# Query norms applied inside the exponential, and attention software-pipelined one block behind three pairs of score banks

## The reference, cut to what matters

```python
def qkv_heads(x, g_norm, p):
    qkv = rms_norm(x, g_norm) @ p['w_qkv']
    q, k, v = jnp.split(qkv, [N_HEADS * HEAD_DIM, (N_HEADS + N_KV) * HEAD_DIM], axis=-1)
    q = rms_norm(q.reshape(bsz, t, N_KV, GQ, HEAD_DIM), p['q_norm'])
    k = rms_norm(k.reshape(bsz, t, N_KV, HEAD_DIM), p['k_norm'])
...
def sink_softmax(s, valid, sink):
    m = jnp.maximum(jnp.max(s, axis=-1, keepdims=True), sink)
    e = jnp.exp(s - m)
    return e / (jnp.sum(e, axis=-1, keepdims=True) + jnp.exp(sink - m))
...
    s = jnp.einsum('bnqkgd,bnskd->bnkgqs', qc, kb) * SCALE     # 64-frame chunk sees itself and the one before
    pr = sink_softmax(s, valid, sink)
    o = jnp.einsum('bnkgqs,bnskd->bnqkgd', pr, vb)
    y = x + o @ p['w_out']
```

## Time and profile before

| what | value |
|---|---|
| median of 3 runs | 1814.18 us (1810.55 to 1814.22) |
| the profiled execution's own time | 1818.81 us |
| its span | 1817.1 us, mean granted TensorE clock 0.933 |
| PE busy | 1654.3 us (91%) |
| DVE, ACT, POOL busy | 727.7, 295.9, 599.8 us |
| chain that ended last | PE 83%, DVE 8%, POOL 3% |

### The profile page before, as it was taken

The page is one execution under the profiler, slowest core; times in us unless marked ns, Lnnn a source line. Parts: engine busy times, 40 slices in busy tenths (PEclk is TensorE's granted clock), DMA queues, the critical chain, the costliest instruction groups (busy, mean ns, idle before and its releaser), DMA issues.

```text
span 1817.1 us, 33445 instructions
## 1 busy us (share of the span) xinstructions
PE 1654.3 (91%) x14584; PEld 1578.1 (87%) x14584; DVE 727.7 (40%) x1256; ACT 295.9 (16%) x483; POOL 599.8 (33%) x356
## 2 busy tenths in 40 slices
PE   6997875887887999999999999976899999999999
PEld 6996764776776999999999999954799999999999
DVE  6645676666664542200222112867243310022100
ACT  3001222221222221100111001133121200012000
POOL 2433234243202333334333343222033433334332
PEclk9997776889997999999999999976699999999999
DMA  7540001000003344444444444430044444444442
GB/s 291 169 162 14 8 16 24 2 15 15 2 15 124 116 142 159 149 152 138 141 160 149 152 139 139 139 116 1 8 156 139 138 139 155 152 156 138 146 161 98
DMA packets 41609, 201.58 MB, mean 111 GB/s; under 512 B 13888, under 2 KB 15040, under 8 KB 19008
## 3 DMA queue, kind: packets, MB, share of 16 engines
q1 hardware_dynamic: 19232, 96.89, 15.4%
q0 software_dynamic: 12528, 91.23, 15.0%
q10 hardware_dynamic: 9744, 11.88, 2.2%
HBM read 192.82 MB, written 6.37 MB: 110 GB/s over the span
## 4 chain that ended last, share of the span: by engine, by line
PE 83%; DVE 8%; POOL 3%; issue 2%; ACT 2%; DMA 1%; ACTq 1%; SPq 0%; DVEq 0%; POOLq 0%
PE PS L587 20%; PE PS L588 20%; PE PS L589 20%; PE PS L562 3%; PE PS L564 3%; PE PS L563 3%; PE PS L680 2%; PE PS L650 2%; PE PS L841 1%; PE PS L620 1%; PE PS L664 1%; PE PS L855 1%; PE PS L859 1%; POOL EE L518 1%; PE PS L611 1%
## 5 line engine op out<-in xcount | busy, mean ns | idle before, releaser
L412 POOL TENSOR_TENSOR WL<-WR,WH 128x2048 fp32r<-128x2048 f32 x87 | 405.7, 4663 | 459.0 <-DMA WH<-in_w 449.5
L587 PE MATMUL PS<-HH,WH 128*128 128x320 f32 x1344 | 416.8, 310 | 3.7 <-POOL WL L412 2.0
L589 PE MATMUL PS<-HH,WL 128*128 128x320 f32 x1344 | 415.9, 309 | 0.0
L587 PE MATMUL PS<-XH,WH 128*128 128x320 f32 x1120 | 347.2, 310 | 0.4
L589 PE MATMUL PS<-XH,WL 128*128 128x320 f32 x1120 | 346.1, 309 | 0.0
L588 PE MATMUL PS<-XL,WH 128*128 128x320 f32 x1120 | 346.1, 309 | 0.0
L588 PE MATMUL PS<-HL,WH 128*128 128x320 f32 x896 | 276.9, 309 | 0.0
L587 PEld LDWEIGHTS PS<-HH,WH 128*128 128x128 f32 x1344 | 252.9, 188 | 5.6 <-issue 3.2
L589 PEld LDWEIGHTS PS<-HH,WL 128*128 128x128 f32 x1344 | 253.0, 188 | 0.0
L587 PEld LDWEIGHTS PS<-XH,WH 128*128 128x128 f32 x1120 | 210.3, 188 | 1.4 <-issue 1.1
L588 PEld LDWEIGHTS PS<-XL,WH 128*128 128x128 f32 x1120 | 210.3, 188 | 0.3
(11 more groups left out here) (389 smaller groups left out, 2295.9 us busy)
## 6 DMA issues: line engine op xcount, KB each, us to landing
WH<-in_w POOLq DMA_DIRECT2D x87, 1024.0 KB, 5.2
WR<-in_w SPq DMA_DIRECT2D x87, 1024.0 KB, 4.9
X<-in_xT SPq DMA_DIRECT2D x8, 320.0 KB, 11.0
out<-X ACTq DMA_DIRECT2D x8, 320.0 KB, 5.0
UR<-UF ACTq DMA_DIRECT2D x16, 80.0 KB, 4.2
UF<-UR SPq DMA_DIRECT2D x64, 20.0 KB, 1.8
WR<-in_wglu SPq DMA_DIRECT2D x1, 1024.0 KB, 4.9
S<-in_s ACTq DMA_DIRECT2D x4, 256.0 KB, 2.6
```

Of the source, the lines that this page charges most:

```text
L412: nc.gpsimd.tensor_tensor(WL[:, r], WR[:, r], WH[:, r].bitcast(F32), ALU.subtract).then_inc(w_split, 2)
L587: mm(out, wh[:, k, wc], xh[:, k, cols], start=(k == 0), stop=False)
L589: last = mm(out, wl[:, k, wc], xh[:, k, cols], start=False, stop=(k == kt - 1))
```

## The change

- The query norm is no longer multiplied into the queries. Their weight goes into the copy of the keys (`KD`), and one over their root into the `scale` operand of the exponential, with a table `RQ` of 20 columns for each of four pairs of query tiles. All query sums take the narrow form (`query_sums`), beside the projection, the last pair after it. For the samples the scale is spread by `query_back` and multiplied in `sample_queries`.
- The value tiles move ahead of the queries in the projection, and their transposes into slot 2 and behind it (`value_rows`).
- `exps` reads the scores from PSUM: four activations of 128 columns, each with a scale and a bias that are columns in SBUF and a sum output (`accum_out`), in place of one of 512. DVE no longer writes the shifted scores, nor reduces the sums. The multiplication by the reciprocal goes from POOL to DVE.
- Scores rotate over three pairs of banks (4/5, 0/1, 2/3); transposes have bank 6 alone and outputs bank 7 alone. PE's turn becomes values of block i-3, transposes of block i-2, scores of block i. The sample blocks stand between prompt blocks 13, 14 and 15.
- `X` is written to DRAM and read back after the attention; `PT`, `VW` and `VS` lie in its room.
- POOL copies the new sample keys, and then loads and splits the weight slot 52, which before it did ahead of the attention.

```diff
-QKV_TILES = [8, 9, 0, 1, 2, 3, 4, 5, 10, 11, 6, 7]
+QKV_TILES = [8, 9, 10, 11, 0, 1, 2, 3, 4, 5, 6, 7]
+ATT_ORDER = list(range(14)) + [16, 14, 17, 15]
...
@@ GpSimd
-            for r in range(AO % 2 + 2):
-                split(r % 2, AO // 2 + r // 2, True)
-            for u in range(UNITS):
-                pool.wait_ge(sm_inv, u + 1)
-                gt(e, e, SM[:, u % 2, 5, 0:ng].unsqueeze(2).broadcast_to((P, ng, kk)), M).then_inc(sm_p, 1)
+            split(0, AO // 2, True)
+            split(1, AO // 2, True)
+            new_keys()
+            split(0, AO // 2 + 1, True)
...
@@ TensorE
+            def query_sums(p):
+                pe.wait_ge(qk_sq, 2 * p + 4)
                 for m in range(2):
                     for t in range(5):
                         at = 10 * m + 2 * t
+                        last = mm(PS[:, 2, at:at + 2], SC[:, m, t * P:(t + 1) * P], BD[:, 0:P:64], start=True, stop=True)
+            def attend(i):
+                if i >= 3:
+                    values(i - 3)
+                if i >= 2:
+                    transposes(i - 2)
+                scores(i)
+            def qkv_attention():
+                slot_as_ready("qkv", XH, XL, KT, xn_wait(3), range(KT), 2)
+                slot("qkv", 1, 1, XH, XL, KT, between=key_sums)
+                slot("qkv", 2, 2, XH, XL, KT, between=lambda n: value_rows(0, NCH if n == 1 else 0))
+                value_rows(NCH, NCH + NB)
+                for i in range(3, N_QKV):
+                    slot("qkv", i, i, XH, XL, KT, between=lambda n: query_gap(i - 3, n))
+                query_sums(3)
+                attend(0)
+                attend(1)
+                query_back()
+                for i in range(2, UNITS):
+                    attend(i)
...
@@ ScalarE
+            def exps(i):
+                act.wait_ge(sm_sub, i + 1)
+                if u < 16:
+                    fn(sm[3][:, 0:4], sm[2][:, 0:4], ACT.Exp)
+                    for g in range(4):
+                        c = 10 * (g % 2) + 2 * (u % 4) + g // 2
+                        last = fn(ee(i)[:, g * P:(g + 1) * P], PS[:, b0 + g // 2, (g % 2) * P:(g % 2 + 1) * P], ACT.Exp,
+                                  bias=sm[1][:, g:g + 1], scale=RQ[:, u // 4, c:c + 1], accum_out=sm[4][:, g:g + 1])
+                    last.then_inc(sm_exp, 1)
...
+                act.wait_ge(unit_done, end_unit("qkv"))
                 act.dma_start(KS[:, :, :, 0:CH], ckT).then_inc(cache_in, 16)
-                act.dma_start(VS[0:CH, :, :], cv).then_inc(cache_in, 16)
+                for k in range(UNITS):
+                    if k >= 3:
+                        out_high(k - 3)
+                    if k >= 2:
+                        transposed(k - 2)
+                    exps(k)
...
+                for k in range(KT):
+                    act.dma_start(X[:, k], XD[:, k]).then_inc(x_in[k], 16)
...
@@ VectorE, less_max and over_sum
                 o(v.tensor_reduce(sm[0], ps, AX.X, ALU.max))
-                o(tt(sm[1], sm[0], sink, ALU.max))
-                tt(sm[2], sink, sm[1], S_)
-                tt(e, ps, sm[1].unsqueeze(3).broadcast_to(shape), S_).then_inc(sm_sub, 1)
+                if u < 16:
+                    o(tt(sm[0], sm[0], RQ[:, u // 4].rearrange("p (a t h) -> p t h a", a=2, h=2)[:, u % 4], M))
+                o(stt(sm[1], sm[0], -1.0, sink, M, ALU.min))
+                if u < 16:
+                    tt(sm[2], sm[1], sink, S_).then_inc(sm_sub, 1)
...
-                o(v.tensor_reduce(sm[4], e, AX.X, A))
                 o(tt(sm[4], sm[4], sm[3], A))
-                v.reciprocal(sm[5], sm[4]).then_inc(sm_inv, 1)
+                o(v.reciprocal(sm[5], sm[4]))
+                tt(e, e, sm[5].unsqueeze(3).broadcast_to(shape), M).then_inc(sm_p, 1)
```

More of the change, by code:

```diff
@@ L589, in slot @@
                             last = mm(out, wl[:, k, wc], xh[:, k, cols], start=False, stop=(k == kt - 1))
-                    last.then_inc(unit_done, 1)
+                        if between:
+                            if h == 1:
+                                last.then_inc(unit_done, 1)
+                            between(2 * j + h)
+                    if not between:
+                        last.then_inc(unit_done, 1)
             def stage(name, xh, xl, kt, wait=None, order=None, L=None):
@@ new lines, in out_high, with qkv_attention @@
+            def out_high(i):
+                act.wait_ge(pv_done, i + 1)
+                ps, dst = o_tiles(i, XHB)
+                fn(dst, ps, ACT.Copy).then_inc(o_hi, 1)
+            def qkv_attention():
+                square(0)
+                square(1)
+                act.wait_ge(x_spilled, 16 * KT)
+                act.wait_ge(xn_lo, 4 * KT)
+                act.dma_start(VS[0:CH, :, :], cv).then_inc(cache_in, 16)
+                key_root(0)
+                key_root(1)
+                value_rows(0, NCH)
+                square(2)
+                value_rows(NCH, NCH + NB)
+                square(3)
+                act.wait_ge(qk_ready, 2)
@@ L1512, in out_high @@
-            def out_high(u):
-                act.wait_ge(pv_done, u + 1)
-                ps, dst = o_tiles(u, XHB)
-                fn(dst, ps, ACT.Copy).then_inc(o_hi, 1)
-            def attention():
-                for i in range(UNITS + 2):
-                    if i < UNITS:
-                        exps(i)
-                    if i >= 2:
-                        out_high(i - 2)
-                    if 0 <= i - 1 < UNITS:
-                        transposed(i - 1)
+                for p in range(3):
+                    query_root(p)
+                    square(4 + 2 * p)
+                    square(5 + 2 * p)
@@ new lines, in out_low, with qkv_attention @@
+            def out_low(i):
+                dve.wait_ge(o_hi, i + 1)
+                ps, dst = o_tiles(i, XLB)
+                _, hi = o_tiles(i, XHB)
+                tt(dst, ps, hi.bitcast(F32), S_).then_inc(o_lo, 1)
+            def qkv_attention():
+                dve.wait_ge(unit_done, unit0("qkv"))
+                v.memset(VP[:, :, 0:CH], 0.0).then_inc(v_pad, 1)
+                qkv_evac(0)
+                qkv_evac(1)
+                qkv_evac(2)
+                key_norm(0)
+                qkv_evac(3)
+                key_norm(1)
+                dup_keys()
+                qkv_evac(4)
+                qkv_evac(5)
+                for p in range(3):
+                    query_inv(p)
+                    qkv_evac(6 + 2 * p)
+                    qkv_evac(7 + 2 * p)
+                query_inv(3)
+                less_max(0)
+                less_max(1)
+                over_sum(0)
+                sample_queries()
+                for k in range(2, UNITS):
+                    if k >= 3:
+                        out_low(k - 3)
+                    less_max(k)
+                    over_sum(k - 1)
+                over_sum(17)
+                out_low(15)
+                out_low(16)
+                out_low(17)
```

380 lines of the change are left out of this document (181 added, 199 removed).

## The result

The changed kernel takes 1823.7 us (median of 5 timed runs, 1822.01 to 1828.35) against 1814.18 for the kernel before. The ratio is 1.0062, 95% interval [1.0043, 1.008]: slower, by 8 to 15 us. Forecast was 1816, no measurable difference. The changed kernel is slower in both.

What follows compares the result with a forecast made beforehand. TensorE alone bounds the projection; in the attention no engine is full and a loop of waits sets the turn. Projection end 1195.2 + attention 100.6 + block 3.7 = 1299.5 against 1297.4, +2: forecast 1816 us, range 1804 to 1825.

Steps and rivals of the forecast that it cites:

- Projection, +5: Projection, TensorE full: wide head sums out -6.45, narrow sums in +7.2, value transposes in +4.3; together +5.0 us.
- Head, -13: From T, the last projection matmul, to the first block's weights: 10.1 us against 23.1 before.
- One turn, 4.69 or 4.34: One attention turn: 4.69 us at TensorE's lower clock, 4.34 at the higher, about 4.6 mixed, against 4.02 before.
- loop A: Turn's loop through maximum, sum, transposes and scores: 4.69 us at the lower clock, 3.75 at the higher.
- loop B: Turn's loop through maximum, exponentials, ACT's high half and DVE's low half: 4.34 us, the longer loop at the higher clock.
- The sum of the attention, 100.6: Preparation and attention: 104.4 us at the lower clock, 100.6 with a quarter of the time higher, against 107.2 before.
- clock higher: Rival, attention: more turns at the higher clock and POOL's split out of the way, -7 us, 1807; chance 0.17.
- The one-time block, +3.7: First attention turns: POOL's split of slot 52 holds a DVE instruction with SBUF operands; +3.7 us, bounds 0 to 5.
- At nothing: Spill and return of `X`, stores of keys and values, `new_keys` on POOL: no cost; a late return at most 5 us.
- the exponentials are no bound: Rival, attention turns: costlier sum outputs make the exponentials the bound, deciding from 2.45 us; 1823; chance 0.20.
- `KS` does not hold ACT: Rival, head: the load of `KS` by itself holds ACT's queue for 8.02 us; +6 us, 1822; chance 0.11.
- The turn did not stay at 4.02: Rival, attention: loops overlap better than drawn and the turn stays at 4.02 us; 9 us come back, 1807; chance 0.12.

Runs made afterwards that it cites:

- e5_halves: Changed kernel with each twenty query head-sum matmuls cut into two halves of ten, an output tile apart: 1818.35 us, ratio 1.0014 to the kernel before.
- e4_one_sum: Changed kernel with one 20-column matmul standing for each twenty head sums of the three query tiles inside the projection: 1815.71 us, ratio 0.9993 to the kernel before.
- e8_order_late: Changed kernel with TensorE's and DVE's turns reordered and POOL's split of slot 52 held until the last values, head sums whole: 1789.99 us, ratio 0.9854.
- e1_split_late: Changed kernel with POOL's load and split of slot 52 held until the values of the 17th block are done: 1815.95 us, ratio 0.9998.
- e2_scores_ahead: Changed kernel with TensorE taking values, scores, transposes, so scores stand ahead of transposes, plus one wait: 1811.48 us, ratio 0.997 to the kernel before.
- a2_again: The changed kernel timed once more, unaltered, beside the kernel before: 1820.99 us, ratio 1.003.
- e3_turn_order: Changed kernel with TensorE taking scores, values, transposes, and DVE taking maximum, sum, low half: 1792.43 us, ratio 0.9862 to the kernel before.
- b1_swap: The kernel before, with the load of `VS` issued ahead of that of `KS`, nothing of the change in it: 1815.53 us, ratio 0.9986.

## Why the prediction was wrong

The mechanisms were mostly right, and the sum came out short because two terms stood on a clock that I had set too high.

- *Projection, +5: the step that failed first.* "TensorE is full here, so its work is added up" counts instructions and assumes that each runs at full speed. The counted part was, if anything, too high: three sums out (-6.45), three in (19 matmuls in 2.12 on the chain, 2.13 for twenty, +6.4), value rows 1.96 + 1.86 = 3.8 for the 4.3 that I took. That is +3.8, and `e5_halves`, with the same matmuls and no fall of the clock, measured +4.0. Put at nothing were one or two falls of the clock at 1.5 us: +5.3 to +6.8 in all, measured 5.6 and 7.1. `e4_one_sum` and `e5_halves` show it. No row of before could show it: the only narrow sums there, line 1073 in the earlier trace rows, stand behind the projection, with no full stretch after them. My upper bound of +7 nearly covered the size, but for another reason, late evacuations, that no trace shows.
- *Head, -13:* held. T + 10.1 was forecast for the first block's weights without the block, and `e8_order_late` has 9.9 with the sums at 2.41. Where the sums ran partly at the lower clock, it was 11.3 (`e1_split_late`), which the forecast did not have. The kernel after, with block and slow sums, has 14.5.
- *One turn, 4.69 or 4.34:* loop A held, loop B was too high. 4.62 at the lower clock with exactly the chain of loop A; 3.92 and not 4.34 at the higher one; and `e2_scores_ahead` laid loop B bare at 3.91. The average of 4.60 that came out as forecast has luck in it: fewer turns at the higher clock than assumed, shorter ones there, and the memsets that I had counted apart. The exponentials took 1.97 for the 2.1 forecast, and the low bound of 0.72 was far off. The Trainium skill's 93 ns for each column operand (ScalarE: Activation LUTs, What ACT_TABLE_LOAD costs) had given 0.17 more; the trace is nearer to the row's figure: 0.44 for an activation of 128 columns with two column operands.
- *The sum of the attention, 100.6: the second term that failed.* It took the clock share of before over. Measured were 0.55 in the turns and 0.50 in the tail, where rows 1 had 0.63 and 0.58. From the first weights on my terms give 104.4 - 10.1 = 94.3 us at the lower clock and 90.5 with a quarter of the time high; measured were 91.7, nearly all low. By the same slope the lost share is worth some 2.6 us and the low-clock terms were some 1.4 too high (both estimates), so one error hid half of the other. This miss is also of the size of the spread between executions: with the same turns `a2_again`, `e4_one_sum` and `e5_halves` measured 91.0, 89.2 and 91.2. The rival "clock higher" had used the same lever in the wrong direction. Its condition, 0.70, was met only by the kernels with the order of `e3_turn_order`.
- *The one-time block, +3.7:* held. One small DVE instruction took 4.3 us too long (4.49 less 0.17), of which 3.2 to 4.3 reached the first weights, inside the bound of 5. Five of the seven DVE instructions of a turn have two operands in SBUF, as the prediction counts, and not four as the section on the change has it. The rule of the Trainium skill (SBUF — State Buffer, Who interferes with whom) fits again: an instruction of 4 columns was held until POOL's was done.
- *At nothing:* the return of `X` and the stages behind cost nothing, 519.7 in both.
- *The rivals:* the exponentials are no bound (1.97, it wanted 2.45). `KS` does not hold ACT: its issue took 0.62 in the kernel after, with the table load right behind. The turn did not stay at 4.02.

Added up for the first pair of traces: +2.1 in the projection and +1.9 in preparation and attention beyond the forecast (block 0.6, clock share and the rest of the turns 1.2), and +3.4 ahead of the projection, within the spread. Behind the projection's start the traces have +3.5 and +6.1 where +2 was forecast: the verdict hung on 1.5 to 4 us, nearly all of it the clock. With the falls gone from the projection (`e5_halves`) the ratio is 1.0014 [0.9999, 1.003], which is no measurable difference, as forecast.

## What to carry to other kernels

Where an in-order queue holds work for several blocks, draw the loop through each queue at once. Here only the places of `scores` and `out_low` cost 33 us of a stretch of 106, together with the clock that came with them, far more than any of the parts that the change moved. Work that is added to a full TensorE is not priced by its durations alone: look for what it does to the granted clock behind it, and try a run of very narrow matmuls in parts, as `e5_halves` does. And a stall that ends a chain is worth only what is left to the next latest arrival: price it by that, not by its length.

## What the runs showed that I had not expected

- The granted clock falls inside a stretch in which TensorE has no gap: behind 20 matmuls of 128x2 (2.1 us), some 3.3 us at 0.5, in 9 cases of 21. With ten of them at a time (1.17 us) it did not, in four traces.
- A tighter loop was repaid twice: attention at 4.62 us a turn had a clock of 0.55, and at 2.5 to 3.0 us one of 1.00 for most of the time, with the same matmuls; which came first is not told apart there, since both start with the first turns. `e2_scores_ahead` shows the first step alone: 3.91 us a turn with the clock still at 0.50.
- An activation that also gives its sum is two records: 0.44 for 128 columns and 0.19 for reading the sum out, together 0.44 from start to start.
- A DMA issue behind one that loads `KS` was held for 8.02 us on ACT's queue; with the order turned, both issues took 0.6 (`b1_swap`).
